# The low part of split weights read last, and three vector steps moved, in a two-block fp32 transformer kernel

## What is computed

```python
# end of the first block
h = h + peer_ffn(rmsnorm(h, ffn_norm), peer_wq, peer_keys, peer_u, peer_v)
gate = sigmoid(rmsnorm(h, ple_gate_norm) @ ple_gate_w)
h = h + (p @ ple_proj) * gate
# second block, for layer in (0, 1)
hn = rms_norm(h, mix_norm_g[layer])
h = h + (even_mixer if layer == 0 else odd_mixer)(hn, ...)   # @ w_in ... @ w_out
hn = rms_norm(h, ffn_norm_g[layer])
u, v = split(hn @ w_up, 2)
uc = conv_b + sum(conv_w[j] * shifted(u, j) for j in range(3))
h = h + (silu(uc) * v) @ w_down          # D_FF = 2816
```

## Time and profile before

| | us |
|---|---|
| three executions | 1691.97, 1695.82, 1697.97 (median 1695.82) |
| profiled execution, its own time | 1691.37 |
| its span in the profile | 1689.6 |
| TensorE busy in the span | 1427.8 (85%) |
| VectorE busy | 994.9 (59%) |
| ScalarE busy | 527.6 (31%) |
| GpSimd busy | 514.7 (30%) |
| mean granted clock of TensorE | 0.974 of full speed |

### The profile page before, as it was taken

The page is one execution under the profiler, slowest core; times in us unless marked ns, Lnnn a source line. Parts: engine busy times, 40 slices in busy tenths (PEclk is TensorE's granted clock), DMA queues, the critical chain, the costliest instruction groups (busy, mean ns, idle before and its releaser), DMA issues.

```text
span 1689.6 us, 17396 instructions
## 1 busy us (share of the span) xinstructions
PE 1427.8 (85%) x6588; PEld 943.1 (56%) x6588; DVE 994.9 (59%) x1811; ACT 527.6 (31%) x820; POOL 514.7 (30%) x550
## 2 busy tenths in 40 slices
PE   7999986877676767776677769999999999999998
PEld 6665655522222222222222227657999888689997
DVE  2245468366556566655554456356788566568863
ACT  3253320311111111211111306564444356444442
POOL 4000025466666666666666640000000000000000
PEclk9899998999999999999999989999999999999999
DMA  9323059699999999999999964423555545246542
GB/s 302 114 100 112 6 213 380 267 409 401 353 372 373 370 367 379 360 372 369 382 379 360 363 220 150 150 100 100 160 189 199 177 162 188 100 150 195 174 181 100
DMA packets 162691, 413.75 MB, mean 245 GB/s; under 512 B 11193, under 2 KB 57515, under 8 KB 162480
## 3 DMA queue, kind: packets, MB, share of 16 engines
q0 software_dynamic: 75632, 272.63, 42.4%
q1 hardware_dynamic: 86656, 138.58, 24.1%
q10 hardware_dynamic: 320, 1.43, 0.2%
HBM read 411.55 MB, written 1.05 MB: 244 GB/s over the span
## 4 chain that ended last, share of the span: by engine, by line
PE 53%; POOL 20%; issue 10%; DMA 7%; DVE 5%; another core or an unknown queue 4%; ACT 2%; POOLq 0%; SPq 0%; DVEq 0%; ACTq 0%
PE ps L1277 15%; POOL arena L2872 9%; PE ps L701 7%; PE ps L1286 7%; PE ps L1037 3%; PE ps L1224 3%; POOL xT L2885 3%; POOL wX L2885 3%; DMA arena<-in_peer_u,routes 3%; POOL mixed L2885 3%; POOL proj L2885 3%; PE ps L1141 2%; PE ps L1020 2%; PE ps L1053 2%
## 5 line engine op out<-in xcount | busy, mean ns | idle before, releaser
L2468 DVE SCALAR_TENSOR_TENSOR arena<-arena,ps 128x1024 f32<-128x1024 f32 x256 | 307.1, 1220 | 241.6 <-DMA arena<-in_peer_u,routes 201.8
L2872 POOL DMA_INDIRECT arena<-in_peer_u,routes x256 | 247.0, 965 | 141.5 <-issue 73.2
L1750 ACT ACTIVATE state<-cst,gatew 128x128 f32<-128x128 f32 x240 | 86.4, 395 | 412.0 <-remote 157.0
L2056 DVE TENSOR_TENSOR w_lo<-ring,w_hi 128x2048 fp32r<-128x2048 f32 x66 | 151.1, 2292 | 86.7 <-ACT w_hi L1870 86.7
L1870 ACT ACTIVATE w_hi<-ring 128x2048 fp32r<-128x2048 f32 x66 | 125.9, 1910 | 146.2 <-issue 67.0
L1141 PE MATMUL ps<-wX,state 128*128 128x512 f32 x240 | 122.4, 634 | 57.6 <-DMA wX<-in_peer_v,routes 41.0
L1141 PE MATMUL ps<-mixed,state 128*128 128x512 f32 x240 | 119.0, 619 | 51.5 <-DMA mixed<-in_peer_v,routes 36.7
L1141 PE MATMUL ps<-xT,state 128*128 128x512 f32 x240 | 120.5, 628 | 45.0 <-DMA xT<-in_peer_v,routes 34.3
L1141 PE MATMUL ps<-proj,state 128*128 128x512 f32 x240 | 119.9, 624 | 44.6 <-DMA proj<-in_peer_v,routes 33.1
L1141 PEld LDWEIGHTS ps<-wX,state 128*128 128x128 f32 x240 | 41.7, 193 | 135.8 <-issue 127.5
L1141 PEld LDWEIGHTS ps<-mixed,state 128*128 128x128 f32 x240 | 41.4, 192 | 128.4 <-issue 124.9
(11 more groups left out here) (464 smaller groups left out, 2339.8 us busy)
## 6 DMA issues: line engine op xcount, KB each, us to landing
ring<-in_ffn_w_up SPq DMA_DIRECT2D x22, 2048.0 KB, 8.8
ring<-in_ffn_w_down SPq DMA_DIRECT2D x10, 2048.0 KB, 7.5
ring<-in_even_w_in SPq DMA_DIRECT2D x7, 2048.0 KB, 7.7
ring<-in_w_in SPq DMA_DIRECT2D x6, 2048.0 KB, 21.1
ring<-in_odd_w_in SPq DMA_DIRECT2D x6, 2048.0 KB, 7.9
ring<-in_peer_wq SPq DMA_DIRECT2D x4, 2048.0 KB, 16.3
ring<-in_w_out SPq DMA_DIRECT2D x2, 2048.0 KB, 7.9
arena<-in_peer_u,routes POOLq DMA_INDIRECT x256
```

The lines of the kernel that those rows point to most:

```text
L1750: do(diags[n % DIAGS], ident, ACT.Copy, scale=gatew[:, u * UROWS + b:u * UROWS + b + 1]).then_inc(diag_ready, 1)
L2056: v.tensor_tensor(w_lo[j % 2][:], w, w_hi[j % 2][:].bitcast(F32), ALU.subtract).then_inc(lo_ready, 1)
L2468: v.scalar_tensor_tensor(row, row, 1.0, token_tile(u // PAIR_UNITS), ALU.mult, ALU.mult, accum_out=dots[:, b:b + 1]).then_inc(u_used, 1)
L2872: pool.indirect_dma_start(arena[:, b % GATHER_SLOTS, :], None, a["peer_u"][0], route_of(u, b))\
```

## The change

On TensorE, a unit now waits for the high part of its weights and runs steps 0 and 2; before the first product with the low part it waits for the low part, and runs step 1 last. That holds for `split_unit`, for `up_part` from chunk 1 on (there each block runs steps 0, 2, 1, and the wait stands in the first block), and for `down_part`. In `first_product` the order stays (steps 0 and 1, then 2), with the wait for the low part behind step 0. The first chunk of `w_up` and the function for the odd mixer's first units (`key_and_queries`) keep order and wait. On VectorE `mix_split(gate + 3)` goes behind `expert_sum(1)` and behind the first `half_turn` and `half_low` of the gate's turn, and `mix_split(even + 1)` goes behind the gate product and the add of the first half. On ScalarE `mix_cast(even + 1)` goes behind the sigmoid of the gate's first chunk. Some bookkeeping changes with it (`stop` flags, buffer indices of equal parity). No transfer, buffer or arithmetic instruction is added or taken away.

```diff
@@ split_unit
-                pe.wait_ge(mix_lo, j + 1)
+                pe.wait_ge(mix_hi, j + 1)
...
-                    for step, (w, x_) in enumerate(((hi, m_hi), (lo, m_hi), (hi, m_lo))):
-                        if step not in steps:
-                            continue
+                    for step in steps:
+                        w, x_ = ((hi, m_hi), (lo, m_hi), (hi, m_lo))[step]
+                        if tile == 0 and step == 1:
+                            pe.wait_ge(mix_lo, j + 1)
@@ out_product, split_product, gate chunk 1, odd mixer chunks 5 and 6
-                split_unit(i, half, (0, 1, 2), True)
+                split_unit(i, half, (0, 2, 1), True)
@@ conv_ffn, down_part
-                    for step, (w, g_) in enumerate(((hi, g_hi), (lo, g_hi), (hi, g_lo))):
+                    for w, g_ in ((hi, g_hi), (hi, g_lo), (lo, g_hi)):
+                        if w is lo and tt == half_ == 0:
+                            pe.wait_ge(lo_ready, j + 1)
@@ conv_ffn, chunks 1 to 10 of w_up
-                        unit_split(FUNITS * layer + 2 * c + u)
+                        j = FUNITS * layer + 2 * c + u
+                        pe.wait_ge(hi_ready, j + 1)
                         for f in range(2):
-                            last = up_part(c, u, f, (0, 1, 2), range(KD))
+                            up_part(c, u, f, (0, 2), range(KD))
+                            if f == 0:
+                                pe.wait_ge(lo_ready, j + 1)
+                            last = up_part(c, u, f, (1,), range(KD))
@@ conv_ffn, down_begin
-                    unit_split(FUNITS * layer + 2 * FCH + c)
+                    pe.wait_ge(hi_ready, FUNITS * layer + 2 * FCH + c + 1)
@@ scalar
             mix_cast(even)
-            mix_cast(even + 1)
...
                 last.then_inc(pair_read[PLAN[i1 + c][0]], 1)
                 if c == 0:
+                    mix_cast(even + 1)
                     half_turn("mix2a", 0)
@@ vector
-            mix_split(gate + 3)
             expert_sum(1)
             for half_ in range(2):
                 half_turn("ple", half_)
                 half_low("ple", half_)
+                if half_ == 0:
+                    mix_split(gate + 3)
...
-            for j in (0, 1):
-                mix_split(even + j)
+            mix_split(even)
             for c in range(2):
...
                 v.tensor_tensor(h[:, :, 512 * c:512 * (c + 1)], h[:, :, 512 * c:512 * (c + 1)], g_, ALU.add).then_inc(h_ready, 1)
+                if c == 0:
+                    mix_split(even + 1)
                 half_turn("mix2a", c)
```

More of the change, by code:

```diff
@@ L691, in split_unit @@
                         for k in range(lo.shape[1]):
+                            ends = last_step and step == steps[-1]
                             if features:
@@ L695, in split_unit @@
                                 o = psf[0:m, 1024 * PLAN[i][0] + T * (2 * half + tile):][:, 0:T]
-                                last = mm(o, w[:, k, tile * P:tile * P + m], x_[:, k, :], start=(step == k == 0), stop=(step == 2 and k == KD - 1))
+                                last = mm(o, w[:, k, tile * P:tile * P + m], x_[:, k, :], start=(step == k == 0), stop=(ends and k == KD - 1))
                             else:
@@ L701, in split_unit @@
                                 last = mm(o, x_[:, k_, tile * P:(tile + 1) * P], row_of(w, k), start=(step == k_ == 0),
-                                          stop=(step == 2 and k_ == KD - 1), skip_group_check=True)
+                                          stop=(ends and k_ == KD - 1), skip_group_check=True)
                 if last_step:
@@ L724, in out_product @@
                 begin(i)
-                split_unit(i, 0, (0, 1, 2), True)
+                split_unit(i, 0, (0, 2, 1), True)
                 half_turn(turn_name, 0)
-                split_unit(i, 1, (0, 1, 2), True)
+                split_unit(i, 1, (0, 2, 1), True)
             def split_product(i):
@@ L1149, in _ @@
             begin(i1)
-            split_unit(i1, 0, (0, 1, 2), True)
+            split_unit(i1, 0, (0, 2, 1), True)
             half_turn("mix2a", 0)
-            split_unit(i1, 1, (0, 1, 2), True)
+            split_unit(i1, 1, (0, 2, 1), True)
             first_product("mix2a")
@@ L1257, in _ @@
             out_product("even_w_out", "ffn2a")
-            def unit_split(j):
-                pe.wait_ge(lo_ready, j + 1)
-                return w_hi[j % 2], w_lo[j % 2]
             def conv_ffn(layer):
@@ L1270, in up_part @@
                 def up_part(c, u, f, steps, ks):
-                    hi, lo = (w[:].rearrange("p (k n) -> p k n", k=KD) for w in (w_hi[(FUNITS * layer + u) % 2], w_lo[(FUNITS * layer + u) % 2]))
+                    j = FUNITS * layer + 2 * c + u
+                    hi, lo = (w[j % 2][:].rearrange("p (k n) -> p k n", k=KD) for w in (w_hi, w_lo))
                     o = psf[:, 1024 * PLAN[i1 + c][0] + 512 * u + T * f:][:, 0:T]
@@ L1277, in up_part @@
                             last = mm(o, w[:, k, f * P:(f + 1) * P], x_[:, k, :], start=(step == k == 0 and not c == 0 < f),
-                                      stop=(step == 2 and k == KD - 1), skip_group_check=(c == 0))
+                                      stop=(step == (1 if c else 2) and k == KD - 1), skip_group_check=(c == 0))
                     return last
                 def down_part(c, tt, half_):
-                    hi, lo = (w[(FUNITS * layer + 2 * FCH + c) % 2][:].rearrange("p (k n) -> p k n", k=2) for w in (w_hi, w_lo))
-                    for step, (w, g_) in enumerate(((hi, g_hi), (lo, g_hi), (hi, g_lo))):
+                    j = FUNITS * layer + 2 * FCH + c
+                    hi, lo = (w[j % 2][:].rearrange("p (k n) -> p k n", k=2) for w in (w_hi, w_lo))
+                    for w, g_ in ((hi, g_hi), (hi, g_lo), (lo, g_hi)):
+                        if w is lo and tt == half_ == 0:
+                            pe.wait_ge(lo_ready, j + 1)
                         for k in range(2):
                             last = mm(ps[:, 4 + 2 * tt + half_, :], g_[:, 2 * c + k, tt * P:(tt + 1) * P], w[:, k, 512 * half_:512 * half_ + 512],
-                                      start=(c == step == k == 0), stop=(c == FCH - 1 and step == 2 and k == 1), skip_group_check=True)
+                                      start=(c == k == 0 and w is hi and g_ is g_hi), stop=(c == FCH - 1 and w is lo and k == 1), skip_group_check=True)
                     return last
@@ L1293, in conv_ffn @@
                 for u in range(2):
-                    unit_split(FUNITS * layer + u)
+                    pe.wait_ge(lo_ready, FUNITS * layer + u + 1)
                     for f in range(2):
@@ L1394, in _ @@
                     begin(i1 + n)
-                    split_unit(i1 + n, 0, (0, 1, 2), True)
+                    split_unit(i1 + n, 0, (0, 2, 1), True)
                     if n == 5:
@@ L1401, in _ @@
                         chunk_outputs(1, GLA_DV, grid(block(3), HH, T), gla_value, outs)
-                    split_unit(i1 + n, 1, (0, 1, 2), True)
+                    split_unit(i1 + n, 1, (0, 2, 1), True)
                 if n == 1:
```

## The result

The changed kernel took 1685.0 us (median of five runs, 1683.74 to 1687.0) against 1695.82 for the kernel before, a ratio of 0.9941, 95% interval 0.9925 to 0.9957. By the ratio that is 10 us less, 7.3 to 12.7. Forecast were 1686.8 and 7.5 less. The profiled execution took 1686.73 with a span of 1684.9, only 4.7 less than the 1689.6 before, because its experts' stage happened to end later. So the profiles are compared by their **tail**, from the end of VectorE's last weighted row to the end of the span: it was 1689.6 - 1002.67 = 686.9 and is 1684.9 - 1005.36 = 679.5, 7.4 less. The span is printed to 0.1 us, and a tail is no more exact than that.

The account below looks back on a forecast made before the run. From the experts' end on TensorE was taken as the bound, so only its idle time could be won: 2.0 + 0.77 + 3.66 + 1.12 = 7.55 us off the four executions' mean of 1694.3, giving 1686.8 us, range 1682 to 1693.

Parts of the forecast that it names:

- Term 1: Experts' end: the residual's sum runs ahead of the gate's last split, so TensorE's transposes start 2.0 us earlier; 1.0 kept for the range.
- Term 2: Gate: its product runs ahead of the even chunk's second split, 2.1 us earlier, of which TensorE can use 0.77.
- Term 3: Start of w_up's chunk 1: TensorE runs high-part products instead of waiting for the low part; 1.83 us per layer, 3.66 together.
- Term 4: Last piece of w_down: high part first, so TensorE skips the stop on the low part; 0.56 us per layer, 1.12 together.
- The new waits: TensorE in split_unit, w_up and w_down: 90 added waits, taken to cost 0; upper bound 192 ns each.
- The small gains only in part: Rival at experts' end and gate: term 1 only 1.0, term 2 0; 5.8 us gained, 1688.5 us; chance 0.13.
- The chase in the next units: Rival in w_up: VectorE makes later low parts late, so term 3 is 0; sum 3.9, 1690.4 us; chance 0.08.
- The bared weight load: Rival on TensorE: each of 90 waits costs up to 0.192 us; 9.7 us slower, 1704.0 us; chance 0.05.

Follow-up runs that it names:

- experiment 7: The kernel before with 720 more TensorE waits, each on a high part of the weights that was long ready; single execution, tail 689.3 us.
- the fillers' pair: Kernel before and changed kernel, each with identity products nobody reads where TensorE waits; tails 682.9 and 674.8 us, ratios to before 0.9972 and 0.9921.
- experiment 11: The changed kernel with one more 512-column VectorE subtraction ahead of each w_up low part from unit 4; C0 to w_down 119.52 us, as without it.

## Why the prediction was right, and where it was off

**The bound.** "What a reordering can bring is TensorE's idle time and nothing else" was right for the kernel at an equal clock: 8.0 measured there, 7.55 forecast. It left out what idle time does to the work behind it: the slower restart, and the clock.

**Term 1**, 2.0 forecast: the idle time gave 2.00 in every run that had the step. The value was taken between 1.0 and 2.0 as if the shorter wait could only lose some of it. It won more, because the stretch at 1.2 GHz was shorter or absent. Windows of 25 us around T (clock third from the end) of before, of the kernel with TensorE's order only, of the changed kernel and of the one with only the sum moved:

```profile
995.00:1020.00 25.00, 17.71 (x63) 12.35 (x64) 12.46 (x20) 5.00 (x10) 1.74 (x2) 0.80 0.19 64
```
```profile
1001.00:1026.00 25.00, 19.00 (x62) 12.00 (x61) 12.86 (x21) 4.16 (x8) 2.14 (x2) 0.73 0.21 76
```
```profile
998.00:1023.00 25.00, 19.56 (x77) 14.21 (x78) 13.96 (x21) 7.09 (x12) 1.29 (x2) 0.93 0.18 62
```
```profile
998.00:1023.00 25.00, 20.32 (x87) 14.58 (x86) 16.87 (x23) 9.16 (x13) 1.51 (x1) 1.00 0.26 89
```

In the six profiles without fillers whose sum stands behind the split the clock over such 25 us was 0.73, 0.73, 0.80, 0.80, 0.86 and 0.86; in the five where it stands ahead 0.86, 0.93, 0.93, 0.93 and 1.00. At half speed for (1 - clock) x 2 x 25 us, that is 10.2 and 3.5 us on the average. In time, T-E over what it is at the full clock (26.74, and 25.89 where the gate's steps are moved as well) was 2.2 to 3.7 in the six and 0.0 to 2.6 in the five, means 2.8 and 1.5. So the term is 2.0 + 1.3 on the average: this is the step of the sum that was mis-sized. The two ends that I kept for it, 1.0 and 2.0, both lie below that. The two groups overlap, so the 1.3 is a mean over few profiles and holds for no single pair; in the first pair it was 0.8.

The open question of the prediction, whether the rise of the clock moves with the work, has an answer in these profiles. Before, the rise came at 1012, 9.3 after R. In the changed kernel R is 2.7 later, and the rise came at 1012 again, 6.7 after R:

```profile
1010.00:1012.00 2.00, 2.00 (x6) 1.52 (x6) 2.00 (x1) 0.00 (x0) 0.00 (x0) 0.50 0.00 0
1012.00:1014.00 2.00, 2.00 (x12) 1.61 (x11) 0.14 (x1) 0.00 (x0) 0.00 (x0) 0.98 0.00 0
```

In all six profiles with the sum behind the split it came 8.9 to 12.0 after R, in the four of the others that had a slow stretch 6.1 to 8.2. The means are 3.4 apart, so the rise moved by the 2.0 of the work and by some more. The fall did not move alike: it came 3.3 after R in the second profile of before and 3.3 and 3.1 after it in the two of the changed kernel. Why the slow stretch was shorter, when it began at the same place, is not shown.

**Term 2**, 0.77 forecast: 0.85. **Term 3**, 3.66: 1.83 in each layer at C0 and C1, as forecast, and 0.06 more behind each, since the first group after a stop takes 1.02 instead of 0.96. **Term 4**, 1.12: what is left of C0-K and C1-end, some 0.7 each, because the restart there costs as well (the pair behind that stop takes 0.54, where 0.454 is the pace). I had taken the stop for the idle time alone. The new waits at 0: 0.001 each.

**The sum** with these is 8.0 + 1.3 = 9.3, and 10 was measured, 7.3 to 12.7. The rest can be chance. One part of it may be real: the waits at C0 that are gone can also bring the clock down, as in experiment 7, the only one of the profiles with that wait in which it was seen there. How often that happens was not measured. The parts alone agree within their intervals: 7.4 (5.1 to 9.8) for TensorE's order, where the fillers' pair gives 5.2, and 4.7 (3.1 to 6.4) for the moved steps, where it gives 2.9 and the clock 1.3.

**The profiled executions against the median.** I forecast from the mean of four executions, 1694.3. The kernel's own spread lies in the experts' stage (R between 1001.1 and 1009.7 on the first chips, 996.4 in one run on the last) and in the clock at O2. The tail is what a pair of profiles can be compared by, to some 0.1 us where the clock does alike. The tail of 679.3 forecast for the changed kernel was met, at 679.5, but by luck, from errors that cancel: 1.4 more from the clock and the restarts, against 1.65 lost at O2 by chance. What the prediction had understood is the idle time: 7.55 forecast, 8.0 at an equal clock.

**The rivals.** The small gains only in part: no, all stretches gave theirs. The chase in the next units: no; experiment 11 shows that there is room for 0.7 us more on each low part. The bared weight load: no, by experiment 7. The Trainium skill's rule in "TensorE: Matmul & The Clock Gate", section "What's actually happening", that the monitor's window "doesn't reset when your kernel starts", agrees with O2-F0 at 24.50 and 26.17 in two executions of one kernel. For term 1 it did not mean the loss of 1.0 that I derived from it: counted from R, the rise came earlier by the 2.0 and more.

**A version that beats both** came out of this: the changed kernel with fillers, 0.9921 of the kernel before in two sets of runs, where the change alone has 0.9941. The intervals of the two overlap, and the tails do not: 674.8 twice against 679.5 twice.

## What to carry to other kernels

Where operands are split into a high and a low part, run every product of the high part first and wait for the low part in front of its own product: it costs next to nothing (0.001 us a wait here), it took away all four stops on a low part in this tail, and it leaves the engine that makes the low parts 1.9 us of room. Price a wait of TensorE of 2 to 3 us with the slower matmuls behind it, 1.3 to 1.7 us here when the clock fell, and where the wait can't go, fill it with products that nobody reads. Compare two profiles by a stretch that the gathers do not reach, and take a second profile of the kernel before you explain a difference of under 2 us.

## What was not expected of the hardware

The clock fell or not in the same place of the same kernel: behind a wait of 2.2 us at O2, seven of the eleven executions profiled without fillers had 26.10 to 26.18 for O2-F0, the other four 24.48 to 24.50. The three with fillers had 24.48 or 24.49. Behind the 3.2 us at O3 it cost 1.3 to 1.7 in all but one (24.50 in experiment 7). A wait of 1.78 us at C0, between dense matmuls, was once enough; waits of 1.67 us at C0 and C1 never were, in fourteen cases.
